# Query weights of a fused layer written as contiguous slabs in DRAM during the scan, and reloaded from there later

## What the reference computes

```
q = (hc @ wq).reshape(PEER_CHUNK, PEER_HEADS, 2, D_HALF)      # 8 heads, 2 x 128
s = jnp.einsum('chsd,hskd->chsk', q, subkeys)
vals, idx = lax.top_k(s, PEER_TOPK)                            # 16 of 128 keys, twice
...
act = jax.nn.gelu(jnp.einsum('chkd,cd->chk', u[ex], hc), approximate=False)
return jnp.einsum('chk,chkd->cd', g * act, v[ex])              # 16 experts a head and token
```

## Time and profile before

| | |
|---|---|
| time, median of 3 runs | 2140.48 us (2136.06 to 2141.0) |
| time of the profiled execution | 2134.94 us |
| its span, first to last instruction | 2133.3 us, mean granted clock 0.978 |
| PE busy | 1811.4 us (85%) |
| DVE busy | 1378.9 us (65%) |
| POOL busy | 1183.5 us (55%) |
| DMA | 657.34 MB, mean 308 GB/s |

### The profile page before, as it was taken

One profiled execution on the slowest core, in us unless ns is written; L12 is line 12 of the kernel. 1 busy time (PEld: TensorE's weight loads), 2 busy tenths in 40 slices (PEclk: granted clock), 3 DMA queues, 4 the chain that ended last, 5 costly groups with the idle time before them and its releaser, 6 DMA issues.

```text
span 2133.3 us, 21588 instructions
## 1 busy us (share of the span) xinstructions
PE 1811.4 (85%) x6378; PEld 955.8 (45%) x6378; DVE 1378.9 (65%) x3520; ACT 647.4 (30%) x1510; POOL 1183.5 (55%) x1543
## 2 busy tenths in 40 slices
PE   7999899999998898889988987777777777777776
PEld 2554446999997653444444432222222222222222
DVE  1269863678777597556665567666766665776654
ACT  3145512355453333222222232222222222222221
POOL 2100012454555276766665677776777777677773
PEclk9999999999999999999999999999999999999999
DMA  7354354454455699999999999999999999999997
GB/s 247 93 172 171 107 172 101 123 142 120 121 142 170 210 397 381 406 390 392 381 376 356 369 399 410 409 409 410 409 409 409 410 409 409 399 409 409 409 409 259
DMA packets 295261, 657.34 MB, mean 308 GB/s; under 512 B 71568, under 2 KB 141296, under 8 KB 295152
## 3 DMA queue, kind: packets, MB, share of 16 engines
q0 software_dynamic: 150336, 552.67, 65.8%
q1 hardware_dynamic: 144816, 103.36, 16.5%
HBM read 633.40 MB, written 22.54 MB: 307 GB/s over the span
## 4 chain that ended last, share of the span: by engine, by line
PE 46%; DMA 20%; POOL 13%; DVE 10%; issue 7%; ACT 3%; SPq 1%; DVEq 0%; POOLq 0%; ACTq 0%
PE banks L1968 16%; DMA arena<-in_peer_v_dram,arena 15%; POOL arena L1570 13%; PE banks L2637 4%; PE banks L1989 4%; DMA arena<-in_peer_u_dram,arena 4%; PE banks L553 2%; PE banks L2552 2%; PE banks L1468 1%; PE banks L1057 1%; DVE arena L1908 1%; PE banks L1092 1%; PE banks L1173 1%; PE banks L1096 1%; PE banks L1158 1%
## 5 line engine op out<-in xcount | busy, mean ns | idle before, releaser
L1968 PE MATMUL banks<-arena 128*128 128x512 f32 x1984 | 959.7, 619 | 256.4 <-DMA arena<-in_peer_v_dram,arena 191.0
L1908 DVE CUSTOM_DVE_ANT_0 arena<-arena,banks 128x1024 f32<-128x1024 f32 x512 | 621.1, 1219 | 323.5 <-DMA arena<-in_peer_u_dram,arena 323.3
L1968 PEld LDWEIGHTS banks<-arena 128*128 128x128 f32 x1984 | 359.5, 194 | 843.5 <-issue 450.6
L1570 POOL DMA_INDIRECT arena<-in_peer_v_dram,arena x504 | 472.0, 937 | 238.3 <-PE banks L1968 122.7
L1570 POOL DMA_INDIRECT arena<-in_peer_u_dram,arena x512 | 481.2, 940 | 185.4 <-issue 135.8
L1623 ACT ACTIVATE arena<-arena 128x128 f32<-128x128 f32 x496 | 190.6, 400 | 722.4 <-PE banks L1968 721.6
L2552 PE MATMUL banks<-arena 128*128 128x512 f32 x224 | 109.1, 593 | 0.8 <-ACT arena L2222 0.7
L2637 PE MATMUL banks<-arena 128*128 128x512 f32 x192 | 85.4, 604 | 5.8 <-issue 5.8
L760 POOL TENSOR_TENSOR arena<-arena 128x512 f32<-128x512 f32 x48 | 52.4, 1123 | 65.6 <-issue 50.0
L1989 PE MATMUL banks<-arena 128*128 128x384 f32 x256 | 85.4, 485 | 0.0
L1925 DVE TENSOR_TENSOR arena<-arena 128x16 f32<-128x16 f32 x32 | 5.7, 177 | 123.2 <-ACT arena L1719 123.2
(11 more groups left out here) (338 smaller groups left out, 2510.2 us busy)
## 6 DMA issues: line engine op xcount, KB each, us to landing
arena<-in_w_mod_dram SPq DMA_DIRECT2D x18, 1024.0 KB, 6.9
arena<-in_peer_wq_dram SPq DMA_DIRECT2D x16, 1024.0 KB, 13.1
arena<-in_w_in_dram SPq DMA_DIRECT2D x27, 512.0 KB, 4.2
arena<-kr_scratch SPq DMA_DIRECT2D x96, 128.0 KB, 3.6
arena<-in_peer_u_dram,arena POOLq DMA_INDIRECT x512, 12.7
arena<-in_peer_v_dram,arena POOLq DMA_INDIRECT x512, 12.9
arena<-in_w_mod_dram SPq DMA_DIRECT2D x3, 2048.0 KB, 12.4
bk_scratch<-arena POOLq DMA_DIRECT2D x8, 768.0 KB, 3.7
```

The costliest lines, as they stand in the source:

```text
L1570: pool.indirect_dma_start(ring[:, j % RING, :], None, table, bass.IndirectOffsetOnAxis(ap=idx[:, hi % 4, j:j + 1].bitcast(U32), axis=0)).t ...
L1908: nc.vector.tensor_tensor_reduce(u_ring[:, j % RING, :], u_ring[:, j % RING, :], h2cur, 1.0, 0.0, ALU.mult, ALU.add, acts[:, h % 2, j:j + ...
L1968: m = nc.tensor.matmul(PO[h][:, :], diag[:, j % 4], v_ring[:, j % RING, 512 * h:512 * h + 512], start=hp == 0 and j == 0, stop=hp == HEADS ...
```

## The change

A new scratch tensor in DRAM, `wq_slabs_scratch`, holds for each head one slab of 128 x 2048 numbers. At the end of `do` for n = 2 to 9, SP issues a transfer from `peer_wq` to the slab of head n - 2, DRAM to DRAM, 1 MB, read in pieces of 1 KB. The late reload reads the slab, 8 KB in one piece for each partition, and SP waits beforehand for all eight slabs. The subkeys' semaphore is merged with that of the first loads; the count waited for (48) is 16 more than theirs.

```diff
+    wq_dram = nc.dram_tensor("wq_slabs_scratch", [HEADS, P, KT * 2 * P], F32, kind="Internal").ap()
...
+        def slab_query_weights(h):
+            sp.dma_start(wq_dram[h].rearrange("p (k n) -> p k n", k=KT),
+                         peer_wq[0].rearrange("(k p) n -> p k n", p=P)[:, :, 2 * P * h:2 * P * h + 2 * P]).then_inc(wq_slabbed, 16)
...
             if n + 2 < NBLK:
                 read_loads((n + 2) // 3, (n + 2) % 3)
+            if 2 <= n < HEADS + 2:
+                slab_query_weights(n - 2)
...
-        sp.dma_start(skn, skey_v).then_inc(subkeys_loaded, 16)
+        sp.dma_start(skn, skey_v).then_inc(cond_loaded, 16)
...
         sp.wait_ge(mixer_output, NT)
+        sp.wait_ge(wq_slabbed, 16 * HEADS)
         for h in range(HEADS):
             if h >= 2:
                 sp.wait_ge(late_queries, 2 * h - 2)
-            sp.dma_start(wq2[h % 2], wq_v[:, :, 2 * P * h:2 * P * h + 2 * P]).then_inc(wq_loaded[h % 2], 16)
+            sp.dma_start(wq2[h % 2].rearrange("p k n -> p (k n)"), wq_dram[h]).then_inc(wq_loaded[h % 2], 16)
...
-        pe.wait_ge(subkeys_loaded, 16)
+        pe.wait_ge(cond_loaded, 48)
```

More of the change, by code:

```diff
@@ L304, in _layer @@
     tri_dram = nc.dram_tensor("tri_scratch", [2 * 2 * NB * TRI], F32, kind="Internal").ap()
+    wq_dram = nc.dram_tensor("wq_slabs_scratch", [HEADS, P, KT * 2 * P], F32, kind="Internal").ap()
     inv_dram = nc.dram_tensor("inv_scratch", [2, 2 * NB * 8, SUB * SUB], F32, kind="Internal").ap()
-    cond_loaded = sem("cond_loaded")
+    cond_loaded = sem("cond_then_subkeys_loaded")
     param_rows_loaded = sem("param_rows_loaded")
@@ L390, in _layer @@
     wq_first, wq_low, wq_high = sem("wq_first"), sem("wq_low"), sem("wq_high")
+    wq_slabbed = sem("wq_slabbed")
     mixer_moved = sem("mixer_moved")
-    subkeys_loaded = sem("subkeys_loaded")
     subkeys_transposed = sem("subkeys_transposed")
```

## The result

The changed kernel is slower: 2148.60 us (median of 15 runs, 2142.73 to 2154.44) against 2139.24 us (15 runs, 2135.84 to 2143.85), a ratio of 1.0046 with a 95% interval of 1.0036 to 1.0055. That is 9.4 us. The prediction said slower with 0.77, and 21.7 us; the measured time lies inside its range, but the size is off by more than a factor of two.

The account below looks back on a forecast made before the run. PE's order was taken to bound the scan and late head steps, gathers the part after 1240 us. Stalls 15.9 plus clock falls 6.4 less 0.6 from the reload gave +21.7 us, a median of 2162 us, range 2145 to 2188.

Parts of the forecast that it names:

- T: Time one slab holds SP's queue in the scan, delaying `w_mod` and the inverses' store; taken as 5.0 us.
- the slacks of the prediction: Scan, six blocks with `w_mod` behind a slab: delay covered before PE's `mod_row`, 1.3 to 3.8 us each, 14.1 together.
- the late head steps: Steps issuing late reloads, set by PE's products and the hand-over, not DMA; forecast to stay 46 to 47 us.
- the reload was the bound: Rival, chance 0.07: PE waits for DMA in late head steps; 8 KB pieces give back 17.6 us, so faster.
- slow copies: Rival, chance 0.13: 1 KB DRAM to DRAM pieces cost much more, T 8 us and up; +73 us at T = 10.
- T is at least 3.8 us: Lower bound for the slab's queue time, from two back-to-back 1 MB small-piece loads landing 3.8 us apart.
- neither working that led to 5.0: Two routes to T: between 3.8 and 7.6 us, nearer the low end; and the skill's HBM copy rate, 207 to 214 GB/s.
- the stalls: PE's waits at `mod_row` in six scan blocks: 6 x 5.0 - 14.1 = 15.9 us.
- four falls: Scan: clock drops after the four stalls above 2.3 us, charged 1.6 us each, 6.4 us; 3 us each at T = 7.6.
- the inverses' path: Scan: the inverses' store, queued behind the slab, delays POOL's spread by T; counted as no extra cost.
- The two waits lie side by side, and I count one: In six scan blocks the late inverses' wait overlaps PE's wait at `mod_row`, so only the latter is charged.
- 3.5 us of slack: covered: Block 5, block 8 alike: slab without `w_mod` makes inverses some 3 us late, within the slack before PE needs them.

Follow-up runs that it names:

- slabs only: Changed kernel, but the late reload reads the original weights in 1 KB pieces as before: 2260.53 us, ratio 1.0032; repeated elsewhere 2146.70 us, ratio 1.0043.
- two slabs: Changed kernel with two slabs issued in each place, the second copy to scratch that nobody reads: 2177.80 us, ratio 1.0176.
- late POOL without DMA: Kernel before, no slabs; POOL clears a small scratch tile seven times before the spread in blocks 3 to 10: 2142.92 us, ratio 1.0019.
- the slab behind the inverses: Changed kernel with each slab issued behind the inverses' reload, large reload pieces kept: 2251.99 us, ratio 1.0002; repeated 2135.45 us, ratio 0.9991.
- a late spread without inputs: Slab behind `w_mod`, ahead of the inverses' store; POOL clears targets twice instead of spreading in blocks 3 to 10: 2140.78 us, ratio 1.0015 to the kernel before.

## Why the prediction was half right

**Right.** The sign and the place: the scan is bound by PE, DMA's order in SP's queue matters there, and the slab ahead of `w_mod` makes PE wait at `mod_row` in the blocks with the smallest slacks. With T = 2.8 the slacks of the prediction leave 1.1, 1.0, 0, 0.4, 0 and 1.5 us; measured are 0.67, 0.89, 0, 0.16, 0 and 1.03. The reload gives back nothing measurable, and the late head steps kept their length; the rival "the reload was the bound" fell, and "slow copies" too.

**The step that failed first: T.** "T is at least 3.8 us" was no lower bound. I had read it off two loads issued 0.83 us apart and took the distance of their landings for the time that one holds the queue. The first of the two is the subkeys' load, with pieces of 0.5 KB (128 numbers in a row) and not the slab's 1 KB, so "a slab reads the same pieces" was a misreading. The same trace had rows that price the right pieces: loads of query weights in 1 KB pieces, each issued while the one ahead was still under way. Issue and time to landing of two of them, before:

```profile
706.59 0.38 SPq L1257 DMA_DIRECT2D arena<-in_peer_wq_dram  x1
707.01 4.19 SPq L1257 DMA_DIRECT2D arena<-in_peer_wq_dram  x1
```
```profile
arena<-in_peer_wq_dram SPq DMA_DIRECT2D x1, 1024.0 KB, 12.0
arena<-in_peer_wq_dram SPq DMA_DIRECT2D x1, 1024.0 KB, 14.6
```

They land at 718.6 and 721.6, 3.0 us apart, and so do the loads beside them (705.9, 708.9 and 711.9; 724.6 and 727.5). Measured, a slab delays what is behind it by 2.8 us, even though it also writes to DRAM; neither working that led to 5.0 holds here. In the sum the stalls were put at 15.9 us and are 2.7 (3.6 in a second profile). With T = 3.0 the prediction's own sum would have given 4.8 us of stalls, no fall of the clock and 4.2 us in all, less than half of what was measured.

**The second: the clock.** The 6.4 us for four falls rested on the same T. No wait for `w_mod` reached 2.3 us, and the profiles of the changed kernel show no fall behind one of them. The falls that they do have stand behind waits that the kernel before has too, and they come and go between executions of one kernel: behind a wait of 1.87 us in block 8 the clock stayed at 1.00 in one profile of the kernel before, and behind 1.88 us it fell in the other. (One profile of slabs only has a fall in a new place, behind a wait of 1.84 us for `AA` in block 4; the other has none.) So the wait's length, in this range, does not say whether the clock falls. With two slabs, where the waits are 3.8 us and more, it fell each time, and the one worked out cost 2.2 us, between the 1.6 and the 3 us of the prediction.

**The third, of the other sign: the inverses' path.** "The two waits lie side by side, and I count one" and "3.5 us of slack: covered" asked only when PE needs the spread, and put this path at nothing. They left out what the spread does while it runs. Two to four us later against PE's order, it lies over DVE's decays, whose pair goes from 0.6 to 1.3 us to 1.2 to 2.3 us, and PE then waits for DVE: 5.5 us in the profile. That the late spread makes the larger part of the loss is shown by three runs: late POOL without DMA loses 4.3 us, the slab behind the inverses loses nothing, and a late spread without inputs brings 8.1 us down to 2.5. Nor do the waits lie side by side: taking the one for `w_mod` away shortens the scan by 2.5 to 5.0 us and leaves 6 over the kernel before. A large overestimate and an omission partly cancelled. That the time lies inside the range is luck: T and the clock were too dear by 19.6 us, and the path put at nothing cost about 6.

The Trainium skill ("SBUF — State Buffer", section "SBUF: two separate sides") says that GpSimd and VectorE share a pair of ports, and that a VectorE instruction with two inputs in SBUF contends with a GpSimd instruction that reads SBUF, as an exclusive lock. The runs agree on the contention and its condition: the decays have two such inputs, a pair grows to as much as 2.30 us beside a reading spread, and stays at 0.60 us beside one that only writes. The length fits a lock, as each of the two then takes about as long as one of POOL's four instructions, 1.1 us. That the engines share ports no run here shows.

Open: how much of the late spread's loss in the changed kernel is the collision and how much would be PE's wait for POOL without it, and what set the length of the stretch behind the scan.

## What to carry to other kernels

Bulk work "in a quiet stretch" goes to the place in the queue where nothing short and urgent is behind it: the same 8 MB cost 8 to 11 us ahead of a 128 KB store and nothing that can be measured behind its reload. When an engine off the critical path gets later, compute not only whether its result is still in time but what it will run beside; if it is GpSimd reading SBUF, look for VectorE instructions with two SBUF inputs. When a delay in a queue is priced from rows, take rows with the same pieces. And before larger pieces are bought with a copy, look for a stretch of the same step without the transfer: the two head steps without a reload, as long as the others, had already said that there was nothing to win.

## What the runs showed of the hardware that was not expected

- A DRAM to DRAM transfer of 1 MB in 1 KB pieces delays the next transfer of its queue by 2.8 us, no more than the 3.0 us between plain loads of that size, and pieces of 8 KB at the source change the kernel's time no more than the comparison can tell (1.0035 against 1.0032 and 1.0043).
- Two slabs delay `w_mod` by more than twice one: waits of 24.5 us in six blocks, where 19.5 were worked out from 2.8 us a slab.
- The clock can fall to 1.2 GHz after a wait of 1.87 us of PE in one execution and not in another of the same kernel (block 8, two profiles of the kernel before), so the number of falls in the scan went from one to three between profiles of kernels with and without slabs (two slabs in each place apart).
